# The first pairs of two up projections in another order, and one token sum made by GpSimd

## What is computed

```
def conv_ffn(h, w_up, conv_w, w_down, buf):
    u, new_buf = causal_dwconv(h @ w_up, buf, conv_w)
    a, g = jnp.split(u, 2, axis=-1)
    return (jax.nn.silu(a) * g) @ w_down, new_buf
```

## Time and profile before

| | |
|---|---|
| median of 3 runs | 2818.09 us (2817.53 to 2819.22) |
| profiled execution | 2817.94 us |
| its span, first to last instruction | 2816.3 us |
| mean granted clock of TensorE | 0.965 of 2.4 GHz |
| TensorE busy with matmuls | 2571.8 us, 91% |
| VectorE, ScalarE, GpSimd busy | 1666.9, 1215.7, 450.5 us |
| share of TensorE in the chain that ended last | 71% |
| share of VectorE in it | 15% |

### The profile page before, as it was taken

The page is one execution under the profiler, slowest core; times in us unless marked ns, Lnnn a source line. Parts: engine busy times, 40 slices in busy tenths (PEclk is TensorE's granted clock), DMA queues, the critical chain, the costliest instruction groups (busy, mean ns, idle before and its releaser), DMA issues.

```text
span 2816.3 us, 50414 instructions
## 1 busy us (share of the span) xinstructions
PE 2571.8 (91%) x19111; PEld 1906.3 (68%) x19111; DVE 1666.9 (59%) x2657; ACT 1215.7 (43%) x1737; POOL 450.5 (16%) x500
## 2 busy tenths in 40 slices
PE   5888898899787798899999999999996999999997
PEld 2666676665565554788887666566664888887664
DVE  8255454405899847888887223433339888885123
ACT  4665656331677723555554111211125555553111
POOL 0312303213445400111111000011100111111000
PEclk9899999999999898999999999999998999999999
DMA  3322222365000032111113111111112111113111
GB/s 129 87 60 65 76 77 87 110 183 165 1 1 1 1 106 96 53 55 56 60 52 112 70 51 36 45 45 52 53 50 92 53 60 56 55 60 128 51 51 61
DMA packets 118106, 190.32 MB, mean 68 GB/s; under 512 B 17505, under 2 KB 84434, under 8 KB 117586
## 3 DMA queue, kind: packets, MB, share of 16 engines
q1 hardware_dynamic: 97218, 167.81, 18.7%
q0 software_dynamic: 3792, 12.58, 1.4%
q10 hardware_dynamic: 16960, 8.16, 1.0%
HBM read 169.92 MB, written 22.76 MB: 68 GB/s over the span
## 4 chain that ended last, share of the span: by engine, by line
PE 71%; DVE 15%; ACT 5%; issue 4%; SPq 4%; DMA 1%; POOL 0%; ACTq 0%; DVEq 0%; POOLq 0%
PE PS L2131 32%; PE PS L2579 27%; ACT xT L963 2%; DVE R L1748 2%; SPq L625 2%; SPq L628 2%; DVE R L1418 2%; PE PS L2111 2%; PE PS L2232 1%; PE PS L2164 1%; DVE R L1727 1%; DVE hT L1423 1%; PE PS L2399 1%; DVE R L1412 1%; PE PS L2330 1%
## 5 line engine op out<-in xcount | busy, mean ns | idle before, releaser
L2131 PE MATMUL PS<-hT,R 128*128 128x344 f16 x4104 | 604.4, 310 | 7.2 <-DVE R L570 5.1
L2131 PEld LDWEIGHTS PS<-hT,R 128*128 128x128 f16 x4104 | 401.5, 98 | 207.9 <-DVE R L570 3.4
L2131 PE MATMUL PS<-R 128*128 128x344 f16 x3276 | 478.2, 309 | 3.6 <-DVE xT L1963 3.6
L570 DVE SCALAR_TENSOR_TENSOR R<-W,R 128x1024 f16<-128x1024 f32 (+1 forms) x102 | 145.4, 1426 | 543.6 <-ACT R L564 543.0
L2131 PEld LDWEIGHTS PS<-R 128*128 128x128 f16 x3276 | 320.4, 98 | 161.1 <-issue 4.1
L564 ACT ACTIVATE R<-W 128x1024 f16<-128x1024 f32 (+1 forms) x102 | 117.6, 1154 | 582.1 <-PE PS L2131 548.3
L2579 PE MATMUL PS<-R 128*128 128x258 f16 x3024 | 346.2, 275 | 16.5 <-issue 16.5
L2579 PEld LDWEIGHTS PS<-R 128*128 128x128 f16 x3024 | 294.9, 98 | 61.3 <-issue 17.0
L1891 DVE SCALAR_TENSOR_TENSOR xT<-xT 128x1024 f32<-128x1024 f32 x176 | 225.5, 1281 | 101.2 <-ACT xT L1348 95.4
L2579 PE MATMUL PS<-hT,HM 128*128 128x258 f16 x2016 | 235.6, 273 | 1.1 <-DVE HM L1913 1.1
L2579 PE MATMUL PS<-hT,R 128*128 128x258 f16 x2016 | 229.2, 273 | 1.4 <-ACT xT L1335 1.4
(11 more groups left out here) (332 smaller groups left out, 3691.4 us busy)
## 6 DMA issues: line engine op xcount, KB each, us to landing
W<-wk SPq DMA_DIRECT2D x154, 512.0 KB, 3.5
W<-wdn SPq DMA_DIRECT2D x32, 704.0 KB, 4.1
xT<-cmp_t SPq DMA_DIRECT2D x256, 64.0 KB, 1.9
xT<-x SPq DMA_DIRECT2D x16, 516.0 KB, 7.3
x_kept_in<-xT SPq DMA_DIRECT2D x16, 516.0 KB, 5.0
xT<-x_kept_in SPq DMA_DIRECT2D x16, 516.0 KB, 5.6
o_y<-hT SPq DMA_DIRECT2D x6, 688.0 KB, 3.4
o_win_s<-state_win POOLq DMA_DIRECT2D x1, 4088.0 KB, 23.9
```

Source lines behind the costliest of these rows:

```text
L570: dve.scalar_tensor_tensor(to[:, n, 1, 0:width], W[:, n, 0:width], UNIT, to[:, n, 0, 0:width], ALU.mult, ALU.subtract).then_inc(w_split, 1)
L2131: ins = pe.matmul(wide(u)[:, m, :], weights[half], src[:, other, m * TW:(m + 1) * TW], start=(first and half == other == 0), stop=(last an ...
```

## The change

It keeps all sums and products and touches the start of both up projections and `body` of pair 0.

- T4 is subtracted by GpSimd, in three instructions at the head of `ffn_rows`, as soon as T2 is there; VectorE no longer does it.
- The gate row of the plain first pair gets buffers of its own, `UG` and `YG`; ScalarE fills them later and VectorE's taps on it move from ahead of pair 0 into `body` of pair 0.
- VectorE does `low_sums(0)` and token lows 2 and 3 ahead of the taps of row 0; the product with the gate row, the weight sums of pair 1 and `low_z(0)` come later in `body`.
- ScalarE does `part_sums(0)` and `hold_first(0)` earlier, and `hold_first(1)`, the weight parts of pair 1 and `high(0)` in another order.

```diff
+        YG, UG = reg(2 * TT, TT), reg(3 * TT, TT + 2)
...
             def ffn_rows(s, tiles, pairs):
+                pool.wait_ge(tf_here, 9 * s + 6)
+                for m, f in enumerate((0, 516, 172)):
+                    at_m = slice(m * 172, (m + 1) * 172)
+                    pool.tensor_tensor(TF[3][:, :, at_m], TF[1][:, :, at_m], rows[:, K4:KD, f:f + 172], ALU.subtract
+                                       ).then_inc(t4_here, 1)
                 copies(0, 0)
...
                 def token_high(turn, b):
-                    act.wait_ge(tf_here, 12 * s + (6, 9, 9, 12)[turn])
+                    if b == 3:
+                        act.wait_ge(t4_here, 3 * (s + 1))
...
                     act.activation(split_in_two(HELD[0]), pair_of_banks(z[q % 2]), ACT.Copy, scale=1 / UNIT
                                    ).then_inc(u4_held, 1)
                     if last:
                         split_high(act, following, width=WCH)
+                    elif first:
+                        token_high(3, 3)
+                        hold_first(1)
...
+                    if first:
+                        part_sums(1)
+                        part_last_sum(1)
+                        high(0)
                     act.wait_ge(c12_here, at(i, 2, n + 1))
...
                 first_row(0)
-                token_high(1, 2)
-                token_high(2, 0)
                 wait_full(act, u + 1)
                 part_sums(0)
+                token_high(1, 2)
+                hold_first(0)
+                token_high(2, 0)
                 first_row(1)
-                hold_first(0)
                 part_last_sum(0)
...
                     joined(UF[0][:, 2:2 + HT], quad, HELD[0]).then_inc(c11_here, 1)
-                    product(q, i)
+                    if first:
+                        low_a(1)
...
                     joined(UF[1][:, 2 + HT:2 + TT], 2, HELD[0]).then_inc(c22_here, 1)
                     if first:
                         token_low(4, 3)
+                        weight_sums(1)
+                        weight_last_sum(1)
+                        dve.wait_ge(u_here, s * (2 + KD) + 2)
+                        wait_emptied(dve, u + 1)
+                        taps(YG, UG, old(1), weight(1), tg_here)
+                        low_sums(1)
+                        product(0, gate=YG)
...
                     joined(UF[1][:, 2:2 + HT], 2, HELD[1]).then_inc(c21_here, 1)
+                    if first:
+                        low_z(0)
...
                 token_low(1, 1)
                 weight_last_sum(0)
+                low_sums(0)
+                token_low(2, 2)
+                token_low(3, 0)
                 dve.wait_ge(u_here, s * (2 + KD) + 1)
                 wait_emptied(dve, u)
                 taps(YF[0], UF[0], old(0), weight(0), y_here)
-                token_low(2, 2)
-                token_low(3, 0)
-                dve.wait_ge(tf_here, 12 * s + 9)
-                sums(3, "t2", "21")
-                low_sums(0)
                 low_last(0)
-                dve.wait_ge(u_here, s * (2 + KD) + 2)
-                wait_emptied(dve, u + 1)
-                taps(YF[1], UF[1], old(1), weight(1), tg_here)
                 over_pairs(dve, body, own)
```

More of the change, by code:

```diff
@@ L1329, in body @@
                                    ).then_inc(u2_held, 1)
-                    if first:
-                        token_high(3, 3)
-                    high(q, i)
+                    if not first:
+                        high(q, i)
                     after("p5")
@@ L1348, in body @@
                     act.activation(YF[0], UF[0][:, 2:2 + TT], ACT.Copy, scale=tap(0)).then_inc(yi_here, 1)
-                    if not last:
+                    if not (first or last):
                         part_last_sum(q + 1, i)
@@ L1964, in joined, with sums @@
                                                     ALU.mult, ALU.add)
+                places = ((0, 688), (516, 344), (172, 860))
+                def sums(b, one, minus):
+                    for m, (f, g) in enumerate(places):
+                        at_m = slice(m * 172, (m + 1) * 172)
+                        block = {"11": rows[:, 0:K4, f:f + 172], "12": rows[:, 0:K4, g:g + 172],
+                                 "21": rows[:, K4:KD, f:f + 172], "22": rows[:, K4:KD, g:g + 172],
+                                 "t1": TF[0][:, :, at_m], "t2": TF[1][:, :, at_m]}
+                        dve.tensor_tensor(TF[b][:, :, at_m], block[one], block[minus], ALU.subtract).then_inc(tf_here, 1)
                 def body(q, i=None, first=False, last=False):
@@ L1976, in body @@
                     joined(UF[0][:, 2:2 + HT], quad, HELD[0]).then_inc(c11_here, 1)
-                    product(q, i)
+                    if first:
+                        low_a(1)
+                    else:
+                        product(q, i)
+                        if not last:
+                            low_a(q + 1, i)
+                            weight_sums(q + 1, i)
+                    after("p7")
+                    dve.wait_ge(u4_held, at(i, 2, n + 1))
+                    if not first:
+                        dve.wait_ge(st_here, at(i, 4, 2 + tiles + 2 * p))
+                    joined(UF[1][:, 2 + HT:2 + TT], 2, HELD[0]).then_inc(c22_here, 1)
                     if first:
                         token_low(4, 3)
-                    if not last:
-                        low_a(q + 1, i)
-                        weight_sums(q + 1, i)
-                    after("p7")
-                    dve.wait_ge(u4_held, at(i, 2, n + 1))
-                    dve.wait_ge(st_here, at(i, 4, 2 + tiles + 2 * p))
-                    joined(UF[1][:, 2 + HT:2 + TT], 2, HELD[0]).then_inc(c22_here, 1)
-                    if not last:
-                        weight_last_sum(q + 1, i)
-                    low_z(q, i)
-                    if last:
-                        split_low(dve, following, width=WCH)
-                    else:
-                        low_sums(q + 1, i)
+                        weight_sums(1)
[5 more added lines that the diff above has]
+                        product(0, gate=YG)
+                    else:
+                        if not last:
+                            weight_last_sum(q + 1, i)
+                        low_z(q, i)
+                        if last:
+                            split_low(dve, following, width=WCH)
+                        else:
+                            low_sums(q + 1, i)
                     dve.wait_ge(yi_here, at(i, 4, 2 * n + 1))
@@ L2024, in ffn_up @@
                 weight_sums(0)
-                for n in range(2):
-                    own.up(dve.memset(UF[n][:, 0:2], 0.0))
+                for row in (*UF, UG):
+                    own.up(dve.memset(row[:, 0:2], 0.0))
                 own.settle()
```

31 lines of the change are left out of this document (14 added, 17 removed).

## The result

The changed kernel takes **2829.39 us** (median of 8 runs, 2824.43 to 2834.91) beside 2818.65 us for the kernel before (8 runs, 2813.78 to 2824.61): a ratio of 1.0037, 95% interval 1.0027 to 1.0047, so 10.4 us slower (7.6 to 13.3). The forecast was 2826.9, with its own band from 2823.5 to 2829.5: the measured median lies at the upper end of that band.

A forecast was written before the change was run, and what follows sets the result against it. VectorE's queue was taken to bound the start of each up projection; 3.2 us of pauses plus 1.2 of clock, 8.8 for two, added to the median 2818.09 gave 2826.9 us (forecast band 2823.5 to 2829.5, range 2816 to 2831).

The forecast's parts named there:

- The port: In pair 0, GpSimd's T4 reading SBUF costs VectorE three turns of 1.5 us, 4.4 us net, giving back 2.35 later.
- Rival A: VectorE keeps the SBUF port while it has a queue, so GpSimd's T4 waits until 1138.8; 2823.1 us; chance 0.14.
- The queues: From pair 0 to P1 of pair 2, TensorE pauses total 15.0 us instead of 11.7, so that P1 comes 3.2 later.
- The 5.1 us ahead: At P2 of pair 1 the new kernel leads by 5.1 us, then gives it back in pair 1's pauses.
- The clock: Lower granted clock after the new pauses, costing on P5 to P4 of pair 0: 1.2 us per up projection, bounds 0 and 2.65.
- Rival C: In each up projection the lower clock costs a whole product or more at full price: 2829.8 to 2832 us; chance 0.12.
- The sum: Pauses 3.2 plus clock 1.2 make 4.4 us per up projection, 8.8 for two, giving 2826.9 us.
- B: VectorE and GpSimd don't hold each other up; pair 2's P1 comes 1.3 us earlier; 2815.5 to 2817.9 us; chance 0.12.
- D: Pair 1's pauses don't come and the 5.1 us lead stays: 2807.9 us; chance 0.04.

The follow-up runs named there:

- the memset: Against the changed kernel: GpSimd's three T4 subtractions became one memset of the same elements, reading nothing, and VectorE made T4 after it; 2820.34 us, one run.
- two further moves: Changed order, T4 on VectorE, plus HELD[1] copied before silu(0), and C21 and product 0 moved earlier; against the kernel before: 2816.03 us, ratio 0.9991.

## Why the prediction was right, point by point

**The port, right in size, wrong in place.** The step said three turns of 1.5 us, less 0.1: 4.4. Measured were 6.59 - 2.44 = 4.15, so 1.26, 1.44 and 1.44 for the three. It was to fall on "a weight sum and the first T3 row"; all three turns fell on T3. Rival A's remark that GpSimd doesn't get in between VectorE's short queued operations held for the 1.6 us of the weight sums, and the turns of the earlier trace rows held for T3. Since low_sums(0) stands behind both, the place didn't matter for the sum. That the price belongs to GpSimd's subtractions and not to the order, the runs with T4 on both engines, with the order alone and with the memset show; that it is the reading of SBUF, and not another property of these instructions, is argued from the memset, which wasn't seen beside T3.

**The queues, right within 0.35 us.** From the start of the tiles, which is 1115.82 in the prediction and 1122.37 in the trace after:

| start of | predicted | measured | idle predicted | idle measured |
|---|---|---|---|---|
| P6, pair 0 | +18.93 | +18.80 | 3.1 | 2.85 |
| P5, pair 0 | +27.78 | +27.57 | 3.5 | 1.65 |
| P6, pair 1 | +42.38 | +42.24 | 1.4 | 1.25 |
| P7, pair 1 | +47.8 | +47.58 | 2.8 | 2.52 |
| P5, pair 1 | +51.9 | +51.64 | 1.4 | 1.24 |
| P1, pair 2 | +57.3 | +56.94 | 2.8 | 2.47 |

The brackets of the profile begin where the last matmul ends, some 0.16 after the next could have begun; the prediction's pauses begin there, so 3.1 stands beside 3.0 rather than 2.85. Each place has the releaser that the step named: low_sums, HELD[1] behind silu and the taps, the join C21 behind the waiting tap, low_a(2). P4 was to be hidden, and is: TensorE's timeline has no pause between P5 of pair 0 and P6 of pair 1. The 5.1 us ahead at P2 of pair 1 were there (5.28 at its start: +38.18 instead of +43.46), and went as said. P1 of pair 2 came 2.9 late instead of 3.2. Of that difference 0.13 is there at P6 of pair 0, where GpSimd's T4 had taken 0.25 less than charged; the rest comes in small pieces on the way. The 1.65 instead of 3.5 ahead of P5 is no miss of the wait: P6 and P7 took 7.12 instead of 5.3, and P5 starts where it was to start.

**The clock, right in sum, wrong in place.** The step said that what falls on P6 or P7 is hidden by the pause before P5, and so it was: 1.7 us there cost nothing. It looked for the cost between P5 and P4 of pair 0, where there was none, and took 1.2 between 0 and 2.65. It came at P1 of pair 2, behind the last pause: 4.38 and 4.48 instead of 2.81, so 1.6 in each projection. The price of 2.65 for a product was too high too: in that product's window the mean granted clock was 0.61, so part of it ran at the upper level. Rival C asked for a whole product at full price and was not what came, although its time, from 2829.8, is nearly the measured one; only the traces tell the two apart.

**The sum.** 3.2 + 1.2 = 4.4 was 2.9 + 1.6 = 4.5 in the first projection and 2.8 + 1.7 in the second: two misses of 0.3 to 0.5 that cancel, which is luck. The mechanism didn't need it, the last tenths of the sum did. Twice that is 8.9 of the measured 10.4; the other 1.5 lies within the interval, and whether it is the last part's 1.7 stays open. One sum of the prediction is off: by its own terms the chance of slower is 0.69, not 0.66.

**The rivals.** B fell with T3's 6.59. D fell with pair 1's four waits, each of the length that the rows of before give. A was half right on the port and its time wasn't reached: GpSimd got in at 1129.8, not after low_sums(0). What the prediction didn't say is how the loss divides. Rival B's sum for the order without the port's price, P1 of pair 2 1.3 earlier than before, is what the order alone then showed (1.27). But B allowed 0 to 1.2 for the clock, and it cost 1.67 and 1.62, so that the gain was none (+0.6 in the traces, no difference in the times): the 8.4 us that the order saves in pair 0 stand against waits that it makes in pair 1, some of which two further moves take away.

## What to carry to other kernels

Before moving a share from VectorE to GpSimd, look at what VectorE has queued at that time. Here each of three subtractions on GpSimd kept VectorE's two-input rows waiting for 1.26 to 1.44 us, more than the 0.87 that the same subtraction takes on VectorE itself; and VectorE had a place where it was waiting anyway, in which its own T4 cost nothing. A pause that is taken out of the first pair is worth only what the next pairs don't take back, so walk each put-off operation to the place where it is now waited for. A short wait far from any pause of the old kernel (P5 behind silu, P7 behind a waiting tap) is often one line's order, and moving that line brought most of the loss back.

## What the runs showed that I had not expected

- The two engines took strict turns in T3 (VectorE 2.31 a row instead of 0.87, GpSimd 2.27), yet GpSimd's first instruction didn't get between three queued VectorE rows of 0.69 us, in every kernel with GpSimd's T4 (its first row is 3.23 long in all seven traces). In the kernel before, a 2-element copy of GpSimd from 1131.54 to 1133.74 did get its turn between two queued token lows of 2.3 us. What decides it was not tried and stays open.
- A product behind the same pause of 2.47 us ran in 2.82 or in 4.48 us in two projections of one kernel, at a granted clock of 1.00 and 0.61, and behind one of 2.21 in 2.82 (copy ahead of silu) or in 4.43 us (order alone, second projection). The same wait can cost 1.6 us or nothing beyond itself, so the clock's part of what the single moves won need not come back in another kernel.
- The table load for silu stood ahead of its wait (from 1144.76, 1.28 us, silu at 1148.33), so it cost nothing.
- Stretches of untouched code differ by some microseconds: the head from 1113.7 to 1122.4, the last part 610 or 611.9, and the part between the projections, 976.1 to 976.8 in ten traces, was 973.0 in the one with the copy ahead of silu. That is more than most edits here move. Without a ruler inside the trace the 0.2 to 0.4 us per projection of the order couldn't have been told from nothing: the times give it as +1.7 with an interval from -0.8 to +4.2.
